# A streamed two-network kernel: weight blocks rounded and split by halves, early convolution taps, a seed read from PSUM, and four changes of order

## The reference, cut to what matters

```python
# FFN: out = (silu(h @ w_gate) * (h @ w_up)) @ w_out
# RWKV, per head:  S_t = S_(t-1) * decay_t + (S_(t-1) a_t) b_t + v_t k_t
# hybrid layer:    p = h @ w_in -> q, kv, gate columns and conv columns a, g
def conformer_conv(u, dw_w, dw_b, ln_w, ln_b, pw_w, pw_b):
    a, g = jnp.split(u, 2, axis=-1)
    y = a * jax.nn.sigmoid(g)
    # depthwise convolution, 256 channels, 31 taps, + dw_b
    y = jax.nn.silu(layer_norm(y, ln_w, ln_b))
    return y @ pw_w + pw_b
```

## Time and profile before

| | |
|---|---|
| median of three runs | 2596.01 us |
| the profiled execution | 2598.18 us |
| its span | 2596.4 us |
| mean granted TensorE clock | 0.986 of full |
| busy DVE, ACT, POOL | 49%, 40%, 31% of the span |
| weight blocks rounded, split | 336 each |

### The profile page before, as it was taken

How to read it: one execution, slowest core, us unless ns; L and a number is a source line. 1 busy time by engine, 2 the same in 40 slices (tenths; PEclk the granted TensorE clock), 3 DMA queues, 4 the chain that set the end, 5 groups by cost and what they waited for, 6 DMA issues and landing times.

```text
span 2596.4 us, 47970 instructions
## 1 busy us (share of the span) xinstructions
PE 2475.2 (95%) x18458; PEld 1984.9 (76%) x18458; DVE 1277.6 (49%) x2008; ACT 1044.6 (40%) x1836; POOL 809.4 (31%) x342
## 2 busy tenths in 40 slices
PE   7999999999999999999999999989999999898998
PEld 6888886877778787787878887878877668676776
DVE  3222224536363637555352222236777774577775
ACT  4222224434343434464342222233346552434762
POOL 3444443242424243223444444422221002233002
PEclk9999999999999999999999999989999999999999
DMA  4232333231313132112333323321110002122002
GB/s 138 94 97 89 105 98 96 63 93 56 97 59 92 57 100 73 57 50 80 103 120 97 96 89 97 105 65 49 57 52 30 1 2 64 42 73 73 18 2 73
DMA packets 52003, 188.43 MB, mean 73 GB/s; under 512 B 5760, under 2 KB 6016, under 8 KB 51712
## 3 DMA queue, kind: packets, MB, share of 16 engines
q1 hardware_dynamic: 50688, 181.74, 22.6%
q10 hardware_dynamic: 1152, 4.26, 0.5%
HBM read 183.88 MB, written 2.10 MB: 72 GB/s over the span
## 4 chain that ended last, share of the span: by engine, by line
issue 72%; POOL 15%; PE 9%; DVE 2%; ACT 1%; POOLq 1%; DVEq 0%; DMA 0%; SPq 0%; ACTq 0%
POOL WLO L2647 15%; PE psum L324 2%; PE psum L325 2%; PE psum L326 2%; PE psum L2385 1%; PE psum L2362 1%; PE psum L2400 1%; DVE psum L2190 1%; PE psum L2368 1%; DVE MX L2472 0%; DVE RN L2081 0%; POOLq L2644 0%; ACT PX L2438 0%; PE psum L2216 0%; DMA RAW<-in_wstream 0%
## 5 line engine op out<-in xcount | busy, mean ns | idle before, releaser
L2647 POOL TENSOR_TENSOR WLO<-RAW,WHI 128x1024 fp32r<-128x1024 f32 x334 | 804.4, 2409 | 1758.8 <-ACT WHI L312 1758.7
L312 ACT ACTIVATE WHI<-RAW 128x1024 fp32r<-128x1024 f32 x336 | 355.4, 1058 | 1027.8 <-PE psum L326 807.1
L324 PE MATMUL psum<-HHI,WHI 128*128 128x512 f32 x848 | 340.2, 401 | 18.5 <-DVE HLO L496 12.1
L325 PE MATMUL psum<-HLO,WHI 128*128 128x512 f32 x848 | 336.6, 397 | 0.0
L326 PE MATMUL psum<-HHI,WLO 128*128 128x512 f32 x848 | 336.4, 397 | 0.0
L324 PE MATMUL psum<-H2HI,WHI 128*128 128x512 f32 (+1 forms) x536 | 199.8, 373 | 14.2 <-DVE H2LO L430 7.4
L324 PEld LDWEIGHTS psum<-HHI,WHI 128*128 128x128 f32 x848 | 160.1, 189 | 59.9 <-issue 12.0
L325 PE MATMUL psum<-H2LO,WHI 128*128 128x512 f32 (+1 forms) x536 | 191.9, 358 | 0.0
L326 PE MATMUL psum<-H2HI,WLO 128*128 128x512 f32 (+1 forms) x536 | 191.4, 357 | 0.0
L325 PEld LDWEIGHTS psum<-HLO,WHI 128*128 128x128 f32 x848 | 160.3, 189 | 38.8 <-issue 1.2
L326 PEld LDWEIGHTS psum<-HHI,WLO 128*128 128x128 f32 x848 | 160.1, 189 | 38.7
(11 more groups left out here) (418 smaller groups left out, 4914.3 us busy)
## 6 DMA issues: line engine op xcount, KB each, us to landing
RAW<-in_wstream SPq DMA_DIRECT2D x336, 512.0 KB, 3.5
X<-in_xT SPq DMA_DIRECT2D x8, 256.0 KB, 6.9
out_T<-OUT SPq DMA_DIRECT2D x4, 512.0 KB, 2.7
W3S<-in_lora ACTq DMA_DIRECT2D x5, 384.0 KB, 3.1
XC<-in_ctxT ACTq DMA_DIRECT2D x1, 1024.0 KB, 5.6
TRIG<-in_trig ACTq DMA_DIRECT2D x1, 960.0 KB, 7.5
FCC<-in_first SPq DMA_DIRECT2D x1, 576.0 KB, 8.7
LVL<-in_levels SPq DMA_DIRECT2D x1, 384.0 KB, 9.1
```

The source lines that it names most:

```text
L312: act.activation(WHI[:, q % 2, :], RAW[:, q % 2, :], ACT.Copy).then_inc(rounded, 1)
L324: pe.matmul(out, tile_of(WHI, slot, u), hi(kt), start=first and last[0], stop=False)
L325: pe.matmul(out, tile_of(WHI, slot, u), lo(kt), start=False, stop=False)
L2647: pool.tensor_tensor(WLO[:, s, :], RAW[:, s, :], WHI[:, s, :].bitcast(F32), ALU.subtract)\
```

## The change

- ACT rounds, and POOL splits, each block in two instructions of 512 columns; `rounded` and `split` count two a block. `half_ready` lets PE start a block when its first half is split, and waits for the second at unit 4: in the first four blocks of each FFN, the LoRA blocks from 1 on, and the input projection's tiles from 2 on. Elsewhere `block_ready` waits for both halves.
- In the input projection DVE does channel tile 0's first operation and eight of its taps ahead (three in tile step 10, after cg0 and a wait for "sd gq2", five in step 11). `taps_vector` then has 21 steps with both tiles, and a loop of eight taps of tile 1 alone, each waiting for the one before.
- `inverse_start` waits for m1 and copies under the mask straight from PSUM, in two halves; `before_k` waits for the second.
- The round's modulation block 6: its turn and two units come before `level_second(5, 1)`, the rest behind `solved(0)` as before.
- `state_step(0, p)` no longer waits for GT.
- At the round's end n0 of both pairs comes ahead of n1.
- The swap of gk moves from tile step 6 to 7, ahead of "sum gq0".

```diff
+        HALVES = slice(0, UNITS // 2 * P), slice(UNITS // 2 * P, UNITS * P)
         def round_block(act, q, i=0, nb=0):
...
-            act.activation(WHI[:, q % 2, :], RAW[:, q % 2, :], ACT.Copy).then_inc(rounded, 1)
+            for half in HALVES:
+                act.activation(WHI[:, q % 2, half], RAW[:, q % 2, half], ACT.Copy).then_inc(rounded, 1)
...
+                if second and u == UNITS // 2:
+                    pe.wait_ge(*second)
...
+        def half_ready(pe, q, i=0, nb=0):
+            pe.wait_ge(split, 2 * q + 1 + i * (2 * nb))
+            return split, 2 * (q + 1) + i * (2 * nb)
...
-        rw_pe += [f"xt{LEVELS - 1}_1", "z_0", "turn2", "y_1", ...
+        rw_pe += ["turn2", f"xt{LEVELS - 1}_1", "z_0", "y_1", ...
...
                 def before_k(p):
-                    pe.wait_ge(*V.at(f"m1b_{p}", i))
+                    pe.wait_ge(*V.at(f"xit0b_{p}", i))
...
-                    pe.wait_ge(*V.at(f"s{n - 2}_{p}" if n >= 2 else f"gt_{p}", i))
+                    if n:
+                        pe.wait_ge(*V.at(f"s{n - 2}_{p}" if n >= 2 else f"gt_{p}", i))
...
+                sixth = modulation(6)
+                some(sixth, 2)
                 level_second(LEVELS - 1, 1)
                 solved(0)
-                whole(modulation(6))
+                whole(sixth)
...
                 def inverse_start(p):
+                    dve.wait_ge(*S.at(f"m1_{p}", i))
                     dve.tensor_copy(d.XIT[:, :, :], ident).then_inc(*V.inc(f"xit_{p}"))
                     dve.wait_ge(*V.at(f"xit_{p}", i))
-                    dve.copy_predicated(d.XIT[:, :, :], rep(LVL[:, LEVELS, :]), d.MA1[:, :, 0:CHUNK]).then_inc(*V.inc(f"xit0_{p}"))
+                    for z, half in enumerate((d.B[2], d.B[1])):
+                        pairs = half.rearrange("p (n c) -> p n c", n=HALF)[:, :, 0:CHUNK]
+                        dve.copy_predicated(d.XIT[:, z * HALF:(z + 1) * HALF, :], rep(LVL[:, LEVELS, :], HALF), pairs)
...
-                return {2: ["sum mq"], 3: ["sum mkv"], 5: ["sum gk"], 6: ["gv tokens", "swap gk"], 7: ["sum gq0"],
+                return {2: ["sum mq"], 3: ["sum mkv"], 5: ["sum gk"], 6: ["gv tokens"], 7: ["swap gk", "sum gq0"],
...
+                if tile == "cg0":
+                    dve.wait_ge(*V.at("cg0"))
+                    dve.wait_ge(*A.at("sd gq2"))
+                    first_tap(dve, L, 0).then_inc(*V.inc("first0"))
+                for n in EARLY_TAPS.get(t, ()):
+                    dve.wait_ge(*V.at(f"early{n - 1}" if n else "first0"))
+                    tap(dve, L, 0, n).then_inc(*V.inc(f"early{n}"))
...
-            with dve.Fori(0, CONV_K - 2) as s:
+            with dve.Fori(0, CONV_K - 2 - AHEAD) as s:
...
+            with dve.Fori(0, AHEAD) as s:
+                dve.wait_ge(*V.before("tap", s))
+                tap(dve, L, 1, s + (CONV_K - 2 - AHEAD)).then_inc(*V.inc("tap"))
...
             for s in range(2):
-                pool.wait_ge(rounded, s + 1)
-                pool.tensor_tensor(WLO[:, s, :], RAW[:, s, :], WHI[:, s, :].bitcast(F32), ALU.subtract).then_inc(split, 1)
+                for z, half in enumerate(HALVES):
+                    pool.wait_ge(rounded, 2 * s + z + 1)
+                    pool.tensor_tensor(WLO[:, s, half], RAW[:, s, half], WHI[:, s, half].bitcast(F32), ALU.subtract).then_inc(split, 1)
```

More of the change, by code:

```diff
@@ L91 @@
 SMALL2_BLOCKS = PW0 // UNITS + 1
+EARLY_TAPS = {10: range(3), 11: range(3, 8)}
+AHEAD = 8
 V0 = SMALL2_BLOCKS * UNITS
@@ L311, in round_block, with product @@
                 act.wait_ge(k.blocks_used, q - 1 + i * nb)
-            act.activation(WHI[:, q % 2, :], RAW[:, q % 2, :], ACT.Copy).then_inc(rounded, 1)
+            for half in HALVES:
+                act.activation(WHI[:, q % 2, half], RAW[:, q % 2, half], ACT.Copy).then_inc(rounded, 1)
         def tile_of(t, slot, u, m=P):
             return t[:, slot, u * P:u * P + m]
-        def product(pe, out, slot, units, hi, lo, last, ready=None):
+        def product(pe, out, slot, units, hi, lo, last, ready=None, second=None):
             mm = None
@@ L525, in first_ready @@
                 pe.wait_ge(*pre.dve.at(f"lo{t}"))
-            block_ready(pe, st.b0)
+            second = half_ready(pe, st.b0)
             product(pe, bank[0], st.b0 % 2, [(u, u) for u in range(KT)], lambda t: HHI[:, t, :],
-                    lambda t: HLO[:, t, :], WHOLE, first_ready).then_inc(k.blocks_used, 1)
+                    lambda t: HLO[:, t, :], WHOLE, first_ready, second).then_inc(k.blocks_used, 1)
             for q in range(1, 4):
-                block_ready(pe, st.b0 + q)
+                second = half_ready(pe, st.b0 + q)
                 product(pe, bank[q], (st.b0 + q) % 2, [(u, u) for u in range(KT)], lambda t: HHI[:, t, :],
-                        lambda t: HLO[:, t, :], WHOLE).then_inc(k.blocks_used, 1)
+                        lambda t: HLO[:, t, :], WHOLE, None, second).then_inc(k.blocks_used, 1)
                 if q == 1:
@@ L792, in lora_tensor @@
             for c in range(1, PRO_BLOCKS):
-                block_ready(pe, st.b0 + c)
+                second = half_ready(pe, st.b0 + c)
                 if c == 7:
@@ L801, in lora_tensor @@
                     ready = lambda t: pe.wait_ge(*N.dve.at(f"lo0_{t}"))
-                product(pe, bank[c % 8], (st.b0 + c) % 2, ALLK, n_hi if raw else h_hi, n_lo if raw else h_lo, WHOLE, ready).then_inc(k.blocks_used, 1)
+                product(pe, bank[c % 8], (st.b0 + c) % 2, ALLK, n_hi if raw else h_hi, n_lo if raw else h_lo, WHOLE, ready, second).then_inc(k.blocks_used, 1)
         def lora_scalar(act, st):
@@ L1816, in __init__ @@
                 self.gate = Stage(k, 2, (), ("gate0", "gate1"), (), GATE2_BLOCKS // 2 - 1)
-                self.taps = Stage(k, 0, (), (), ["first0", "first1"])
-                self.tap = Stage(k, 0, (), (), ["tap0", "tap1"], CONV_K - 2)
+                self.taps = Stage(k, 0, (), (), ["first1"])
+                self.tap = Stage(k, 0, (), (), ["tap0", "tap1"], CONV_K - 2 - AHEAD)
+                self.tap_late = Stage(k, 0, (), (), ["tap"], AHEAD)
                 self.tap_out = Stage(k, 0, (), (), ["conv0", "conv1"])
@@ L1870, in win_steps @@
                         dve += [tile]
+                    if tile == "cg0":
+                        dve += ["first0"]
+                    dve += [f"early{n}" for n in EARLY_TAPS.get(t, ())]
                 return pe, act, dve
@@ L1974, in win_tensor @@
                 if t >= 2:
-                    block_ready(pe, st.b0 + t)
+                    second = half_ready(pe, st.b0 + t)
                     for at, n, b in L.parts_of(t):
@@ L1978, in win_tensor @@
                             pe.wait_ge(*L.norm.st.dve.at(f"lo1_{KT - 1}"))
-                        mm = product(pe, bank[b][:, 0:n], (st.b0 + t) % 2, ALLK, *tokens_of(at, n), WHOLE)
+                        mm = product(pe, bank[b][:, 0:n], (st.b0 + t) % 2, ALLK, *tokens_of(at, n), WHOLE, None, None if at else second)
                     mm.then_inc(k.blocks_used, 1)
@@ L2057, in win_scalar @@
                         act.activation(dst, RW[:, tile_at % 4, T:], ACT.Copy).then_inc(*A.inc(f"ctx {name}"))
+        tap_span = lambda L: T if L.last else SPAN
+        tap_bank = lambda L, i: two_banks[2 + i][:, 0:tap_span(L)]
         def win_vector(dve, L):
@@ L2629, in _ @@
                 for s in range(2):
-                    sp.wait_ge(split, i * 2 + (s - 1))
+                    sp.wait_ge(split, i * 4 + 2 * (s - 1))
                     sp.dma_start(RAW[:, s, :], wstream[i * 2 + s]).then_inc(raw_full[s], 16)
@@ L2641, in _ @@
             for s in range(2):
-                pool.wait_ge(rounded, s + 1)
-                pool.tensor_tensor(WLO[:, s, :], RAW[:, s, :], WHI[:, s, :].bitcast(F32), ALU.subtract).then_inc(split, 1)
+                for z, half in enumerate(HALVES):
+                    pool.wait_ge(rounded, 2 * s + z + 1)
+                    pool.tensor_tensor(WLO[:, s, half], RAW[:, s, half], WHI[:, s, half].bitcast(F32), ALU.subtract).then_inc(split, 1)
             with pool.Fori(1, nblocks // 2) as i:
                 for s in range(2):
-                    pool.wait_ge(rounded, i * 2 + (s + 1))
-                    pool.tensor_tensor(WLO[:, s, :], RAW[:, s, :], WHI[:, s, :].bitcast(F32), ALU.subtract)\
-                        .then_inc(split, 1)
+                    for z, half in enumerate(HALVES):
+                        pool.wait_ge(rounded, i * 4 + (2 * s + z + 1))
+                        pool.tensor_tensor(WLO[:, s, half], RAW[:, s, half], WHI[:, s, half].bitcast(F32), ALU.subtract).then_inc(split, 1)
         @block.tensor
```

40 lines of the change are left out of this document (24 added, 16 removed).

## The result

The changed kernel takes 2565.70 us in the median of four runs (2561.53 to 2567.31), against 2595.82 for the kernel before: the ratio is 0.9876, with a 95% interval from 0.9862 to 0.9891. It is 30.1 us faster; the forecast was 26, and 2570. The profiled execution takes 2564.87, 33.3 less than that of before (2598.18).

What follows compares the result with a forecast made beforehand. PE, busy 95% of the span, bounds the kernel; six groups of its waits hold 41.7 us at most. Terms -3.1 -1.6 -0.7 -0.3 +0 -3.0 +2.0 +0 -2.95 -4.4 -5.0 -7.0 give -26: 2596.0 to 2570, range 2561 to 2587.

Steps and rivals of the forecast that it cites:

- The convolution: Input projections: early taps shorten PE's waits for the convolution, -4.4 us in layer 0 and -5.0 in layer 1.
- rival 3: Layer 1's early taps end 2.5 us late and the clock stays low behind both remaining waits: 2580 to 2584; chance 0.15.
- The clock behind the three waits: Behind both convolution waits and layer 1's gk wait, half clock becomes full: -7.0 us, bounds -7.0 and -1.7.
- GT: In the round, state_step(0, 1) starts 0.75 us sooner without the wait for GT: -3.0 us in four rounds.
- Turn 2: Modulation turn ahead of level_second(5, 1) waits for ROWS, +0.5 us a round: +2.0; bounds -0.8 x 4 and +2.6.
- The seed: The inverse's start, copied from PSUM: the wait moves in front of before_k, 0 us, bounds -0.3 and +1.3 a round.
- rival 2: At the seed, POOL's halves start before the identity copy, which waits 1.2 us each round: +5, 2575 us; chance 0.12.
- The halves: Weight blocks: input projections -3.1, LoRA -1.6, FFN's fifth blocks -0.7, start -0.3 us; nothing in the other 320 blocks.
- The second block of the input projections: PE starts on its first half, 1.55 us sooner once a layer: -3.1 us in all.
- POOL's half: Time for POOL to split half a block: taken at 1.25 us, against 2.41 for a whole split.
- The LoRA blocks: Two waits for split blocks, 2.7 us together, ACT's tanh and sigmoid unmoved behind them: -1.6 us, bounds -2.9 and -0.8.
- Rival 1: Every one of 336 weight blocks costs PE 0.1 to 0.18 us, 34 to 60 us in all: slower; chance 0.05.

Runs made afterwards that it cites:

- e4: The changed kernel with each block rounded and split in quarters of 256 columns instead of halves, PE starting at two of four: 2570.32 us.
- e1: The kernel before with only the halves (rounding and splitting in two instructions a block, and half_ready): 2581.36 us.
- e3: The changed kernel with PE waiting for both halves of every block, rounding and splitting still in halves: 2571.96 us.
- e8: The changed kernel with seed from MA1, turn 2 as before, modulation block 1 ahead of level_first(1, 1), and level_first(5, 1) ahead of masked_values(0): 2548.97 us.
- e10: The changed kernel with four early convolution taps in place of eight: 2570.43 us.
- e5: The changed kernel with the seed copied from MA1 again, under one mask copy, and before_k waiting for m1b: 2557.31 us.

## Why the prediction was right, point by point

**What it got right.** The time (2570 against 2565.7) and the steps that carry it. The convolution: a lone tap of layer 0 starts 0.18 us behind the one before and takes 1.04, one of layer 1 0.18 and 0.75, against the forecast 1.20 and 0.92; cg1's product, which now waits for half a POOL subtraction at most, takes 0.89 in layer 1 (2.51 before); layer 0's wait is gone and layer 1's is 0.96 where 1.1 was worked out. DVE after:

```profile
1898.36 1.04 DVE L2215 SCALAR_TENSOR_TENSOR psum<-CIN,VEC,psum 128x783 f32<-128x783 f32 x1 [0.18 <-DVE psum L2215]
...
2295.35 3.91 DVE L2215 SCALAR_TENSOR_TENSOR psum<-CIN,VEC,psum 128x512 f32<-128x512 f32 x5
2299.30 0.89 DVE L2144 TENSOR_TENSOR CIN<-RW 128x512 f32<-128x512 f32 x1
...
2335.43 0.75 DVE L2215 SCALAR_TENSOR_TENSOR psum<-CIN,VEC,psum 128x512 f32<-128x512 f32 x1 [0.18 <-DVE psum L2215]
...
2337.68 1.98 PE L2259 MATMUL psum<-CACC,SQC 128*128 128x512 f32 x4 [0.96 <-DVE CACC L2239]
```

The early taps of layer 1 end at 2299.26, when cg1's product starts: they fill the gap with nothing over, as said, and rival 3 (pushed by 2.5) stayed away: ACT's copy that the product waits for ends at 2299.27. In layer 0 cg1's product got only 0.4 shorter (2.56 to 2.13), where up to 1.2 was hoped for; nothing hung on it.

The clock behind the three waits came as forecast (-7.1 for -7.0). The reason given for it was thinner than it looked: the earlier trace rows shows one seed wait of the kernel before, at 642.9, with full clock behind it, but behind the same wait of 2.26 us in the first round, and in the third, the granted clock was 0.50. That shorter waits would leave the clock up was thus a guess; it held in the three stretches that it was made for.

```profile
508.93:512.34 3.41, 3.39 (x40) 2.63 (x40) 0.95 (x2) 0.60 (x1) 0.00 (x0) 0.50 0.37 131
```

The order in the round: GT brought 0.80 a round for 0.75. Turn 2 waits for ROWS, which ACT copies behind TS, and costs 0.65 a round where +0.5 was taken:

```profile
527.72 0.36 ACT L1120 ACTIVATE ROWS<-psum 4x256 f32<-4x256 f32 x1
...
528.13 0.60 PE L895 MATMUL psum<-SQC,ROWS 4*128 4x4 f32 x4 [0.95 <-ACT ROWS L1120]
```

The seed, against the kernel before, is neutral because the wait moved in front of `before_k`, step by step as worked out: DVE, POOL, PE.

```profile
499.55 0.38 DVE L1263 COPY XIT<-FCC 128x512 f32<-128x512 f32 x1
500.08 0.78 DVE L1268 COPY_PREDICATED XIT<-LVL,psum 128x256 f32<-128x256 int32 x2 [0.15 <-DVE XIT L1263]
...
499.60 2.69 POOL L2692 TENSOR_TENSOR WLO<-RAW,WHI 128x512 fp32r<-128x512 f32 x2 [7.74 <-ACT WHI L317]
...
501.01 1.96 PE L861 MATMUL psum<-AR,KTL 64*64 64x128 f32 x32 [2.15 <-DVE XIT L1268]
```

The identity copy starts at 499.55, the first POOL half at 499.60, and the copy isn't held (0.38 us), so rival 2 didn't happen, by 0.05 or 0.06 us in each of the four rounds. That is luck rather than foresight. That the first to issue wins is what the Trainium skill (SBUF — State Buffer, "Who interferes with whom") says, and both orders have now been seen: 0.38 with the copy first, 0.85 in e4 with POOL first. PE then waits 2.15.

**What was mis-sized.** *The halves.* They were forecast at -5.7, with nothing on DVE but 0.3 at the start and 1.2 in cg1's product. By themselves they bring 16 us (e1), 4 to 6 of it through the early start (e3). The step that failed is "in the other 320 blocks the extra 0.1 us lies on ACT and POOL: nothing". The extra cost is indeed small; what was left out is that the shorter POOL instruction also lets DVE go sooner, at the seed by 1.3 us in every round. Shorter waits also kept the clock up behind FFN's fifth block and layer 1's second (3.0 us), but not in e1 as a whole, whose mean granted clock in the profiled execution is that of the kernel before (0.986). In the sum for the whole change this hid, because the seed from PSUM took the same 1.2 us a round away again: 0 was the right number for a gain and a loss that I had not told apart.

*The second block of the input projections.* Forecast -1.55 each, measured -0.9 in layer 0 and -1.4 in layer 1; the step that failed in layer 0 is that POOL's first half is all that PE waits for. ACT, POOL, PE, and last the wait at FFN's fifth block:

```profile
1735.27 1.15 ACT L317 ACTIVATE WHI<-RAW 128x512 fp32r<-128x512 f32 x2 [3.42 <-PE psum L333]
...
1737.07 0.87 ACT L2056 ACTIVATE SQ<-psum 128x512 f32<-128x512 f32 x2
...
1735.98 3.84 POOL L2692 TENSOR_TENSOR WLO<-RAW,WHI 128x512 fp32r<-128x512 f32 x3 [27.40 <-ACT WHI L317]
...
1738.04 0.50 PE L331 MATMUL psum<-H2HI,WHI 128*128 128x512 f32 x1 [2.69 <-ACT SQ L2056]
...
39.48 0.50 PE L331 MATMUL psum<-HHI,WHI 128*128 128x512 f32 x1 [1.59 <-POOL WLO L2692]
```

POOL's first half is split at 1737.3, but PE starts at 1738.04, behind ACT's SQ copy, which ends at 1737.94 and which PE waits for as well. The row of before named POOL alone, as the last to come. Under it stood the wait for SQ, whose copy ended at 1743.6 in that trace, 0.5 us behind the 1743.1 from which PE was to start: the next to be late, and the forecast had not looked for it.

*POOL's half* was taken at 1.25 and is 1.29 in the median.

*The LoRA blocks* gave 2.7, as much as the two waits together (one of 0.33 is left); the tanh chain that I let half of it go to did not show up. *Clock behind other waits*: FFN's fifth block waits 1.59 and layer 1's second block 1.79 (1.86 and 3.20 before), and both stretches behind them are now at 1.00, 3.0 us that I had in no term.

*Readings that don't hold as written.* The copy from PSUM at 503.15, set against the 2.88 us from MA, ran while POOL was idle, so that pair of rows doesn't show what POOL does; the rows under e1 do, with the same answer. The wait of 3.56 was counted for both layers' second blocks, though layer 1's is 3.20. Layer 0's convolution is put at -4.4 for a wait of 4.2. And rival 3's time doesn't follow from its terms: 2570 + 2.5 + 5.3 is 2578, and the 2 to 6 us for the loop start up to its 2580 to 2584, and with them the range's 2587, have no row behind them. The measured time didn't come near that end.

**Rival 1** (each block pays) is excluded by e1 and e4: doubling the instructions once more costs 5 to 6 us, not 34.

## What to carry to other kernels

A long POOL instruction can hold a DVE operation with two SBUF inputs for its whole length: cutting it in two can pay even where nobody waits for its result, and the row to look for is a DVE operation of the same form with two lengths. When a wait is to be removed, look which instruction uses the same buffer next: reading PSUM for longer moved the wait to the next writer. And price the parts of a change one by one against each other's presence; two steps of 1.2 us a round with opposite signs looked here like one step of nothing, and undoing the losing one and turn 2, with two changes of order, gave 13 to 17 us more (e8).

## What the runs showed of the hardware

A POOL subtraction of 128 rows takes 0.19 us plus 2.15 ns a column (0.74, 1.29 and 2.40 us for 256, 512 and 1024). It can hold a DVE operation with two SBUF inputs for its length (2.88 or 2.91 us for 0.74 with whole blocks, 1.57 with halves), and did not hold the copies under the mask that read PSUM beside it (0.70, or 0.78 for the pair of halves). Where the identity copy came first, by 0.05 us (499.55 and 499.60), it was POOL's half that lasted longer, 1.46. The granted clock fell behind a wait of 2.4 us in the kernel before and stayed at full behind one of 2.48 in e10; of four equal seed waits of 2.26 in one trace, two were followed by half clock and two were not. Repeated executions of one kernel differ by up to 12 us (e5), the slower with the lower mean granted clock (0.988 against 0.995).
